# Prompt attention on one core: the outputs of an older unit issued ahead of the transposes of the next one

## What is computed

```
s = einsum('bqhd,bkhd->bhqk', q, k) * (A_HEAD_DIM ** -0.5) + bias
s = where(k_valid, s, -inf)
p = softmax(s, axis=-1)
o = einsum('bhqk,bkhd->bqhd', p, v)
```

## Time and profile of the kernel before

| | |
|---|---|
| median of 3 runs | 2878.54 us (2876.82 to 2880.29) |
| the profiled execution, its own time | 2877.13 us |
| span of its trace | 2875.3 us |
| TensorE busy | 2718.2 us, 95% of the span |
| VectorE, ScalarE, GpSimd busy | 989.2, 808.8, 970.4 us |
| prompt stage A, first scores to the stream's first transposes | 716.5 to 807.3 us |
| prompt stage B, likewise | 2128.2 to 2229.3 us |

### The profile page before, as it was taken

One profiled execution on the slowest core, in us unless ns is written; L12 is line 12 of the kernel. 1 busy time (PEld: TensorE's weight loads), 2 busy tenths in 40 slices (PEclk: granted clock), 3 DMA queues, 4 the chain that ended last, 5 costly groups with the idle time before them and its releaser, 6 DMA issues.

```text
span 2875.3 us, 47712 instructions
## 1 busy us (share of the span) xinstructions
PE 2718.2 (95%) x18872; PEld 2567.4 (89%) x18872; DVE 989.2 (34%) x1579; ACT 808.8 (28%) x1285; POOL 970.4 (34%) x632
## 2 busy tenths in 40 slices
PE   5999999999788999999999999999988899999998
PEld 4999999999456899999989999997865699999997
DVE  2120225311556622012442212253855663211234
ACT  1221222322543422122232212223245523211222
POOL 2333333333311433333333333333137333333331
PEclk8999999999899999999999999998989999999998
DMA  9222222132375122222212222222130612222221
GB/s 150 80 84 63 74 82 72 58 108 70 131 253 201 57 75 81 73 73 76 78 51 73 87 67 73 84 62 50 45 96 2 154 55 59 79 81 66 73 83 57
DMA packets 396198, 239.63 MB, mean 83 GB/s; under 512 B 14432, under 2 KB 371024, under 8 KB 396112
## 3 DMA queue, kind: packets, MB, share of 16 engines
q1 hardware_dynamic: 396112, 238.48, 29.2%
HBM read 223.46 MB, written 14.98 MB: 83 GB/s over the span
## 4 chain that ended last, share of the span: by engine, by line
PE 87%; DMA 3%; issue 3%; POOL 2%; ACT 2%; DVE 2%; SPq 0%; ACTq 0%; DVEq 0%; POOLq 0%
PE ps L1267 75%; PE ps L1277 3%; DMA raw<-in_ffn_w_gate 1%; PE ps L1371 1%; PE ps L1384 1%; POOL wl L547 1%; PE ps L1414 1%; PE ps L1335 1%; PE ps L1361 1%; PE ps L1444 1%; PE ps L1428 1%; DVE big L936 1%; PE ps L1465 0%; POOL big L607 0%; ACT wh L689 0%
## 5 line engine op out<-in xcount | busy, mean ns | idle before, releaser
L547 POOL TENSOR_TENSOR wl<-raw,wh 128x1024 fp32r<-128x1024 f32 (+1 forms) x296 | 776.0, 2622 | 1570.7 <-ACT wh L689 1570.7
L1267 PE MATMUL ps<-xh,wh 128*128 128x320 f32 x3488 | 794.4, 308 | 32.2 <-POOL wl L547 31.7
L1267 PE MATMUL ps<-xl,wh 128*128 128x320 f32 x3488 | 792.5, 308 | 0.0
L1267 PE MATMUL ps<-xh,wl 128*128 128x320 f32 x3488 | 792.2, 308 | 0.0
L689 ACT ACTIVATE wh<-raw 128x1024 fp32r<-128x1024 f32 (+1 forms) x298 | 335.5, 1126 | 1073.3 <-PE ps L1267 967.8
L1267 PEld LDWEIGHTS ps<-xh,wh 128*128 128x128 f32 x3488 | 583.4, 188 | 34.8 <-issue 34.2
L1267 PEld LDWEIGHTS ps<-xl,wh 128*128 128x128 f32 x3488 | 583.9, 188 | 0.0
L1267 PEld LDWEIGHTS ps<-xh,wl 128*128 128x128 f32 x3488 | 583.9, 188 | 0.0
L907 DVE SCALAR_TENSOR_TENSOR big<-big,ps 128x640 f32<-128x640 f32 x88 | 72.3, 822 | 875.8 <-PE ps L1267 852.9
L1267 PE MATMUL ps<-hh,wl 128*128 128x320 f32 x1408 | 319.5, 308 | 0.0
L1267 PE MATMUL ps<-hh,wh 128*128 128x320 f32 x1408 | 319.5, 308 | 0.0
(11 more groups left out here) (220 smaller groups left out, 2165.0 us busy)
## 6 DMA issues: line engine op xcount, KB each, us to landing
raw<-in_ffn_w_gate SPq DMA_DIRECT2D x88, 512.0 KB, 3.9
raw<-in_ffn_w_up SPq DMA_DIRECT2D x88, 512.0 KB, 3.9
raw<-in_ffn_w_down SPq DMA_DIRECT2D x64, 704.0 KB, 4.4
a_kc<-in_cache_a_k SPq DMA_DIRECT2D x16, 1024.0 KB, 5.6
a_vc<-in_cache_a_v SPq DMA_DIRECT2D x16, 1024.0 KB, 5.2
raw<-in_a_w_in SPq DMA_DIRECT2D x24, 512.0 KB, 3.7
raw<-in_b_w_in SPq DMA_DIRECT2D x16, 512.0 KB, 3.8
skewed<-big SPq DMA_DIRECT2D x1, 5248.0 KB, 55.7
```

The source lines that it names most:

```text
L547: nc.gpsimd.tensor_tensor(wl[s][:, 0:kt, :], raw[s][:, 0:kt, :], wh[s][:, 0:kt, :].bitcast(F32), ALU.subtract).then_inc(w_lo[s], 1)
L1267: mm = nc.tensor.matmul(ps[:, 2 * s + c, 0:TH], w[:, k, :], x[:, k, TH * c:TH * (c + 1)], start=k == 0 and j == 0, stop=k == kt - 1 and j ...
```

## The change

On TensorE, in step u of the prompt attention of both stages, O of unit u - 4 is issued ahead of T of unit u - 3, where it stood behind it. Nothing else changes: no instruction is added or removed, no wait differs, and the orders of the other engines stay.

```
--- before.py
+++ after.py
@@ -1394,10 +1394,10 @@
                 for u in range(NU + 4):
                     if u < NU:
                         scores(u)
+                    if u >= 4:
+                        outputs(u - 4)
                     if 3 <= u < NU + 3:
                         turn_probs(u - 3)
-                    if u >= 4:
-                        outputs(u - 4)
```

## The result

| | before | after |
|---|---|---|
| median of 12 runs each | 2877.3 us (2875.54 to 2884.95) | 2888.27 us (2883.61 to 2895.0) |
| ratio | 1 | 1.0036 (95%: 1.0027 to 1.0045) |
| span of the trace | 2875.3 us | 2885.5 us |

The change makes the kernel slower by 10.4 us (7.8 to 13.0; the ratio times 2878 us). The forecast was 4.4 us more, and the measured time lies above the range's end of 2886.7. The span grew by 10.2 us, so the profile holds about the whole loss.

A forecast was written before the change was run, and what follows sets the result against it. Stage A's rounds were taken as bound by a loop through ScalarE's copy of T0, stage B's by slope table, bias, inverse, scaling. Rounds cost 0, two tails 2.2 us each: 2878.54 + 4.4 = 2882.9 us, range 2879.3 to 2886.7.

The forecast's parts named there:

- The wait that O might fill: Stage A rounds: the 0.77 us wait moves from T1 to O0, keeping its size; stage B's waits move likewise; gain 0.
- rival 4: Rounds of both stages: GpSimd's scaling is the wait, as the page says, so the kernel gets faster, 2861 us; chance 0.04.
- The cover of the copies: Between T and O of one unit: VectorE's copies stay hidden with 0.07, 0.10 and 0.15 us to spare; cost 0.
- rival 1: Stage A, ahead of O1 and O2: copies uncovered, each 0.1 us beyond the spare costs 1.4 us; total 5.8; chance 0.13.
- Shapes: O straight after S on TensorE: 0 extra taken, bounded by one fixed part of a block, 0.15 us either way.
- rival 2: O1 and O2 after S in stage A: a fixed part more each, 2.1 us, total 6.5, 2885.0 us; chance 0.09.
- The tail's waits: Last steps of each stage, without S: TensorE waits for VectorE's copies ahead of O29, O30, O31; 2.2 us a stage.
- What the tail delays: Stream behind each stage: the last O releases it, so the whole shift counts and 0 of it is hidden.
- rival 3: Streams behind the tails: bound by their transfers, they take half or all of the shift; 2878.5 to 2880.7 us; chance 0.10.
- the sum of the tail: From O28 to O31's first load in each stage: steps and copies in bare succession, 6.45 us, 2.18 more than before.
- some tenths of a us: Stage B: one round's granted clock was 0.85 on the mean; a round like that more or less widens the range.

The follow-up runs named there:

- The experiment with ScalarE's copy: Old TensorE order, ScalarE copying turned probabilities of u - 3 between the two exponentials of u, against before: -3.7 us (-6.3 to -1.2), ratio 0.9987.
- The steady order: New order in all steps with scores (u < 32), old order in the last four, against before: +0.9 us (-1.7 to 3.5), ratio 1.0003.
- the waits filled: Changed kernel plus one unread matmul behind each of T29, T30 and T31 in both stages; against before +4.6 us (2.0 to 7.2), ratio 1.0016.
- the tails alone: New order only in the last four steps (u = 32 to 35) of both stages, against before: +8.1 us (4.6 to 11.2), ratio 1.0028.
- stage A alone: New order in stage A only, old order in stage B, against before: +4.6 us (2.0 to 7.2), ratio 1.0016.
- two edits that followed the copies and the loop: Old TensorE order, against before: ScalarE's copy ahead of its second exponential, -3.7 us; VectorE's inverse ahead of the bias in stage B, -9.5 us.

## Why the prediction was wrong, step by step

- *The wait that O might fill*: right. It moved to O0 and nearly kept its size (0.68 for 0.77), stage A's round is 9.33 for 9.36. The experiment with ScalarE's copy confirms what ends it, so the page's releaser (rival 4) fell.
- *The cover of the copies*: right in stage A but for 0.05 us at O1, where 0.07 were to spare; 7 rounds of it are 0.35 us, and the next wait takes them. In stage B the step was wrong in place and right in price: VectorE's idle time stands ahead of the bias, the copy comes behind the bias and `take_output`, and O1 waits some 0.7 us in six rounds, in slack. The steady order together costs 0.9 us (-1.7 to 3.5), so rival 1 is not seen: its 1.4 us lie inside that interval, but stage A's round did not grow.
- *Shapes* (rival 2): fell. O2 follows S2 in the same 0.85 us as T3 followed it, and O1 is 0.05 us late where the rival wanted 0.15.
- *The tail's waits*: right to 0.1 us. 0.61 + 0.74 + 0.88 = 2.23 us a stage, and with the waits filled and the clock held 4.6 us (2.0 to 7.2) for both.
- *What the tail delays*: right. The hand-over keeps its 0.79 us, and the stream's next transfer starts 2.61 us behind it in both traces (809.90 - 807.29 in the earlier trace rows, 810.60 - 807.99 in after), so the whole shift is passed on and rival 3 falls. The transfer is only 0.70 us later in the two profiles, because stage A began 2.0 us earlier in that of after.
- *The term that failed* is the sum of the tail: it took every TensorE step in it at its duration in the rows of before, that is at the full clock, and the stream behind it too. The prediction named the clock only for a round of stage B, and at "some tenths of a us"; neither the 2 x 2.2 us nor the range has a term for the clock of a tail. But the new waits are idle time of TensorE, and its granted clock fell behind them. The fall cost 2.51 us in stage B's tail of after (9.12 for 6.61), and in its stage A's stream 3.45 - 2.46 = 0.99 us on the first transposes.

Together 4.46 + 2.51 + 0.99 = 8.0 of the span's 10.2 us. The two traces can be compared part by part (us, each from its first TensorE instruction to that of the next):

| | before | after | difference |
|---|---|---|---|
| ahead of stage A's first scores | 716.5 | 714.5 | -2.0 |
| stage A | 90.8 | 93.5 | +2.7 |
| stage A's stream, to its last cache transposes | 88.8 | 89.6 | +0.8 |
| from there to stage B's first scores | 1232.2 | 1235.5 | +3.4 |
| stage B | 101.1 | 105.8 | +4.7 |
| from its hand-over to the end | 646.0 | 646.6 | +0.6 |

So 8.2 us lie where the change was priced. The other 2 us are a balance of parts whose instructions are the same in both kernels. Of the 3.4 us, 0.8 is a longer wait for a transfer at the end of stage A's stream (3.0 for 2.2 us). Most of the rest goes with the clock: behind that wait the lower level lasts from 911.1 to 917.9 in before and from 912.3 to 922.5 in after (stretches of before, then of after, granted clock third from the end), and from 2000 on it lasts 13.7 us where before has 10.2:

```profile
911.20:917.80 6.60, 5.03 (x24) 4.15 (x17) 5.35 (x11) 0.00 (x0) 0.00 (x0) 0.50 0.00 0
918.00:922.40 4.40, 4.40 (x32) 4.40 (x31) 4.29 (x8) 0.00 (x0) 0.00 (x0) 1.00 0.02 4
```

```profile
912.40:922.40 10.00, 8.42 (x61) 7.15 (x62) 6.64 (x13) 0.00 (x0) 0.00 (x0) 0.50 0.00 0
```

Whether the change brings this about is open. The same part is 4.1 us longer than in before in the profile of the tails alone, which is half of its 8.1 us, and 4.3 us in that of the filled tails, there all of it near 2000 us; in the other six kernels it is between 0.2 us shorter and 1.5 us longer, and the shortest is stage A alone, which has the same tail of stage A. How often stage B's tail falls to the lower clock can't be told from one profile a kernel. Nor is it settled by what path stage A's bare tail, at 1.00 itself, leads to a fall 10 us later.

## What to carry to other kernels

An order that takes work from between two waits of TensorE costs the waits, and then it may cost the clock. Price the end of a stage, where nothing is left to interleave, at both levels of the granted clock, and look for the fall at the next long wait too, not only in the tail. And a wait's name in the page's groups is a first guess: of two edits that followed the copies and the loop as the timeline shows them, both gained.

## What the runs showed of the hardware

In stage B's bare tail a stand of TensorE of 1.36 to 1.45 us and one of 0.61 us, with two short blocks between, came just ahead of a fall of the granted clock from 1.00 to 0.50 in two of three kernels; in the third, with the same stands, it held. Six transposes that take 0.87 us at 1.00 took 1.54 us behind the fall. An unread matmul in each stand kept the clock at 1.00, with the tail's length unchanged at 6.61 us. A wait of 2.2 to 2.9 us for a transfer cost the clock in three of three kernels whose tail some 10 us earlier was bare, and in none of five others.
